# Gate A moved into earlier stages and two selection lists counted by ScalarE, in one inference step of a hybrid encoder

## The reference, cut to what matters

```python
mod = silu(c) @ w_ada + b_ada                       # 6 x 1024 values for each of two conditions
h = rms_norm(x) * (1 + sc1) + sh1
u, q, k, v, qi, ki, wi, gate_a, gate_b = split(h @ w_in)      # gate_a, gate_b: 1024 wide each
y_ssm = s5_scan(u, ...)                             # A: state space model
score = sum_h w[t,h] * relu(qi[t,h] . ki[s])        # indexer; the 256 highest keys of a query are kept
attn = attention over the keys kept                 # B
out_a = glu_val * sigmoid(glu_gate)                 # from gelu(y_ssm) @ w_glu
out_b = attn @ w_attn_out
x = x + g1 * ((sigmoid(gate_a)*out_a + sigmoid(gate_b)*out_b) @ w_out)
x = x + g2 * hier_moe(rms_norm(x) * (1 + sc2) + sh2)          # 16 experts, two for a token
```

## Time and profile before

| what | value |
|---|---|
| median of 3 runs | 1735.23 us (1731.95 to 1743.67) |
| the profiled execution's own time | 1734.8 us |
| its span, from the first to the last instruction | 1733.0 us |
| mean granted clock of TensorE | 0.92 |
| busy, of the span: TensorE / VectorE / ScalarE / GpSimd | 1460.3 / 886.4 / 336.5 / 169.5 us |
| moved to and from memory | 196.83 MB, mean 114 GB/s |

### The profile page before, as it was taken

The page is one execution under the profiler, slowest core; times in us unless marked ns, Lnnn a source line. Parts: engine busy times, 40 slices in busy tenths (PEclk is TensorE's granted clock), DMA queues, the critical chain, the costliest instruction groups (busy, mean ns, idle before and its releaser), DMA issues. The chain is left out here.

```text
span 1733.0 us, 18606 instructions
## 1 busy us (share of the span) xinstructions
PE 1460.3 (84%) x6385; PEld 814.6 (47%) x6386; DVE 886.4 (51%) x1799; ACT 336.5 (19%) x721; POOL 169.5 (10%) x356
## 2 busy tenths in 40 slices
PE   7799995978755999999988989989972899999870
PEld 1455541446422666666655666544442444444430
DVE  1322224977598989899985555323335111111117
ACT  3311111012462111111113556001110111111110
POOL 0000003020100111111110000000000122222220
PEclk9899997988966999999999999899985899999985
DMA  9200006640104222211004000432227366675728
GB/s 338 98 5 5 4 10 203 201 78 2 32 4 134 62 62 62 62 57 57 37 17 161 2 2 1 180 125 109 100 100 258 137 242 218 244 266 193 261 103 309
DMA packets 135629, 196.83 MB, mean 114 GB/s; under 512 B 27109, under 2 KB 102565, under 8 KB 135221
## 3 DMA queue, kind: packets, MB, share of 16 engines
q1 hardware_dynamic: 121634, 156.23, 27.4%
q0 software_dynamic: 9312, 28.59, 4.5%
q10 hardware_dynamic: 4612, 11.05, 1.8%
HBM read 154.81 MB, written 39.03 MB: 112 GB/s over the span
## 5 line engine op out<-in xcount | busy, mean ns | idle before, releaser
L1075 PE MATMUL ps<-hT,gt_w 128*128 128x352 f32 (+1 forms) x768 | 240.0, 471 | 18.9 <-DMA gt_w<-in_w_glu 18.9
L1109 DVE TENSOR_SCALAR_CACHE_REDUCE tk_hits<-sc,tk_cand 128x384 bf16<-128x384 f32 (+6 forms) x217 | 250.4, 1154 | 7.7
L1930 PE MATMUL ps<-ex_wgu,ex_xT 128*128 x416 | 191.1, 614 | 18.6 <-SPq L1845 10.7
L1075 PEld LDWEIGHTS ps<-hT,gt_w 128*128 128x128 f32 x768 | 146.8, 191 | 108.9 <-DMA gt_w<-in_w_glu 20.0
L1930 PEld LDWEIGHTS ps<-ex_wgu,ex_xT 128*128 128x128 f32 x416 | 79.4, 196 | 113.6 <-issue 113.6
L1490 PE MATMUL ps<-hT,mergedT 128*128 128x512 f32 (+1 forms) x288 | 120.3, 601 | 5.2 <-DMA op_wr<-in_w_route_expert 5.2
L1075 PE MATMUL ps<-zT,gt_w 128*128 128x352 f32 (+1 forms) x384 | 120.9, 468 | 0.0
L2003 DVE SCALAR_TENSOR_TENSOR ex_hid<-ex_silu,ex_weight,ps 128x256 f32<-128x256 f32 x26 | 12.5, 480 | 207.9 <-ACT ex_silu L1975 207.9
L1951 PE MATMUL ps<-ex_wd,ex_hidT 128*128 x208 | 93.6, 593 | 0.2 <-DVE ex_hidT L2010 0.2
L1075 PEld LDWEIGHTS ps<-zT,gt_w 128*128 128x128 f32 x384 | 73.0, 190 | 44.1
L1490 PEld LDWEIGHTS ps<-hT,mergedT 128*128 128x128 f32 (+1 forms) x288 | 50.9, 186 | 68.9 <-issue 63.0
(11 more groups left out here) (425 smaller groups left out, 1867.5 us busy)
## 6 DMA issues: line engine op xcount, KB each, us to landing
ex_wgu<-in_w_gate SPq DMA_DIRECT2D x16, 1024.0 KB, 5.9
ex_wgu<-in_w_up SPq DMA_DIRECT2D x16, 1024.0 KB, 11.1
ex_wd<-in_w_down SPq DMA_DIRECT2D x16, 1024.0 KB, 13.0
sp_ada_w<-in_w_ada SPq DMA_DIRECT2D x14, 1024.0 KB
gt_w<-in_w_in SPq DMA_DIRECT2D x16, 512.0 KB, 5.1
cb_y<-y_dram ACTq DMA_DIRECT2D x16, 512.0 KB, 8.5
merge_left_dram<-qiT SPq DMA_DIRECT2D x8, 544.0 KB, 6.2
mg_gb<-gate_b_dram SPq DMA_DIRECT2D x8, 544.0 KB, 3.7
```

Source lines behind the costliest of these rows:

```text
L1075: i = nc.tensor.matmul(m.ps[:, seq % 8, 0:n], w[:, c % NB, at + k, :], rhs[:, k, lo:lo + n], start=k == 0, stop=k == nk - 1)
L1109: return v.tensor_scalar(hits[0:r, 0:w], m.sc[0:r, c:c + w], scalar, 0.0, ALU.is_ge, ALU.add, accum_out=cnt[0:r, j:j + 1])
L1930: j = nc.tensor.matmul(m.ps[:, 2 + b, :], xT[:, b, k, :], wgu[:, bass.ds(at, 1), k, :].rearrange("p o n -> p (o n)"), start=k == 0, stop=k ...
```

## The change

Three parts.

1. Gate A. Column blocks 0 to 3 are worked out in `ssm_parameters`, 4 to 6 in `index_scores`, block 7 stays. A new class does it: SP loads the block's weights (512 KB), TensorE makes three spans of eight products, ScalarE copies each span from PSUM, GpSimd stores it in a new tensor in memory. The selection stage loads a block's 1088 columns again, and ScalarE takes their Sigmoid at once. To make room, the 16 modulation chunks use one PSUM bank, each as four groups of 64 columns on four strips of 32 partitions; the score groups of the index stage use seven banks, and TensorE waits with each group for all but three of the Relus before it. Half-products of four (one span is two halves) stand after 18 of the 25 score groups.

2. Selection. The lists are put in the order prompt blocks 3 to 7, block 2, sample; VectorE counts the first five, ScalarE the last two, by Sign(candidate - score) with a summing output, turned into a count by two one-column steps. Since a score that equals the candidate counts half there, the two thresholds are mended after the loop (`mended`). The loop of 31 is written out, counts don't wait for one another, and ScalarE makes the last scaling of each mask, after all its evacuations. Count i stands in ScalarE's list behind unit (6.5 i + 4) / 10.2.

3. Experts. The gate and up weights of a place are loaded when the gate and up products that used it are done, the down weights when the down products are.

The core of the diff, by stage and engine. In `ssm_parameters`, SP (the first load stands behind the five rows and log_dt, the second behind the loads of C and D) and GpSimd:

```diff
+                gates.load(sp, 0)
...
+                gates.load(sp, 1)
                 for i in range(2, len(ada)):
                     sp.wait_ge(aps, i - 1)
                     load_mod_weights(sp, i)
+                    if i == 7:
+                        gates.load(sp, 2)
+                    if i == 10:
+                        gates.load(sp, 3)
...
+                for s in range(len(gates.spans)):
+                    gates.store(pool, s)
+                gates.all_stored(pool)
```

TensorE there (`filler(spans, chunks)` takes a span of gate A and a chunk in turn):

```diff
+                def mod_chunk(i):
+                    pe.wait_ge(awl[i % 2], 32 * (i // 2 + 1))
+                    if i:
+                        pe.wait_ge(aev, i)
+                    for k in range(KD):
+                        for x in range(4):
+                            nc.tensor.matmul(m.ps[32 * x:32 * x + 2, 7, 0:AC // 4], m.cT[:, k, :],
+                                             aw[:, i % 2, k, AC // 4 * x:AC // 4 * (x + 1)], start=k == 0, stop=False)
+                    for x in range(4):
+                        j = nc.tensor.matmul(m.ps[32 * x:32 * x + 2, 7, 0:AC // 4], m.ones[DEC:DEC + 1, 0:2],
+                                             ab[:, i % 2, AC // 4 * x:AC // 4 * (x + 1)], start=False, stop=True)
+                    j.then_inc(aps, 1)
...
-                mod_chunks(range(0, 1))
+                filler(range(0, 1), range(0, 2))
                 pe.wait_ge(ldp, 1)
...
-                mod_chunks(range(1, 4))
+                filler(range(1, 5), range(2, 6))
...
-                mod_chunks(range(4, 8))
+                filler(range(5, 8), range(6, 10))
                 pe.wait_ge(wtr, 1)
                 input_matrices(range(0, 6))
-                mod_chunks(range(8, 12))
+                filler(range(8, 12), range(10, 13))
                 pe.wait_ge(bbr, 1)
                 input_matrices(range(6, 8))
...
                     if x == 2:
-                        mod_chunks(range(12, len(ada)))
+                        filler((), range(13, len(ada)))
```

ScalarE copies in the same order, each chunk's row in four parts: span 0 and chunks 0 and 1 ahead of its Exp and Sin, all others behind them. VectorE waits ahead of the decay table, whose place holds the weights of gate A until then:

```diff
+                dve.wait_ge(gates.psum, len(gates.spans))
                 step(v.tensor_copy(m.decay[:, :, :], bc(m.r8[:, :], 2, COLS)))
```

The new class (its `copy` on ScalarE waits for the products and for the store two spans before; its `store` on GpSimd waits for the copy):

```diff
+class GateSpans:
...
+    def load(self, engine, u):
+        if u >= 2:
+            engine.wait_ge(self.psum, 3 * (u - 1))
+        c = OFF_GA + self.columns[u] * P
+        engine.dma_start(self.w[:, u % 2, :, :], self.src[:, :, c:c + P]).then_inc(self.loaded[u % 2], 16)
+
+    def products(self, pe, s, bank, part=range(KD)):
+        _, lo, n = self.spans[s]
+        if part[0] == 0:
+            if s % 3 == 0:
+                pe.wait_ge(self.loaded[(s // 3) % 2], 16 * (s // 6 + 1))
+            if s:
+                pe.wait_ge(self.copied, s)
+        for k in part:
+            i = self.nc.tensor.matmul(self.m.ps[:, bank, 0:n], self.w[:, (s // 3) % 2, k, :], self.m.hT[:, k, lo:lo + n],
+                                      start=k == 0, stop=k == KD - 1)
+        if part[-1] == KD - 1:
+            i.then_inc(self.psum, 1)
```

In `index_scores`, SP and TensorE:

```diff
+        halves, quads = 2 * len(gates.spans), len(steps) // 4
+        half_after = {4 * ((x + 1) * quads // (halves + 1)) + 3: x for x in range(halves)}
...
                 sp.dma_start(m.vs[:, 0:CB, :], A.cache_v[0].rearrange("(b p) d -> p b d", p=P)).then_inc(ld, 16)
+                gates.load(sp, 0)
+                gates.load(sp, 1)
                 sp.wait_ge(m.fst, 64)
...
-                    if n % 4 == 0 and n >= 8:
-                        pe.wait_ge(rl, n - 4)
+                    if n % 4 == 0 and n >= 4:
+                        pe.wait_ge(rl, n - 3)
...
+                    if n in half_after:
+                        x = half_after[n]
+                        gates.products(pe, x // 2, 7, range(KD // 2 * (x % 2), KD // 2 * (x % 2 + 1)))
```

In `select_keys_and_gates`, ScalarE (`gates(u)` evacuates the three or four parts of unit u):

```diff
+                def count(i):
+                    act.wait_ge(cr, i + 1)
+                    for x in range(2):
+                        r, c, w, mc = lists[V + x]
+                        nc.scalar.activation(m.mask[0:r, mc:mc + w], m.sc[0:r, c:c + w], ACT.Sign, scale=-1.0,
+                                             bias=cand[0:r, V + x:V + x + 1].bitcast(F32),
+                                             accum_out=signs[0:r, x:x + 1]).then_inc(sg, 1)
+                    act.wait_ge(sg, 2 * i + 2)
+                    for x in range(2):
+                        k = nc.scalar.activation(cnt[:, V + x:V + x + 1], signs[:, x:x + 1], ACT.Identity,
+                                                 bias=middle[:, x:x + 1], scale=-0.5)
+                    k.then_inc(sc_, 1)
+
+                for u in range(len(units)):
+                    gates(u)
+                    for i in counts_after[u]:
+                        count(i)
+                for j, (r, c, w, mc) in enumerate(lists):
+                    act.wait_ge(mk_, j + 1)
+                    nc.scalar.activation(m.mask[0:r, mc:mc + w], m.mask[0:r, mc:mc + w], ACT.Copy, scale=-NEG).then_inc(done, 1)
```

VectorE's iteration there, in place of the hardware loop (the candidates count for ScalarE as soon as `cr` says so, and its counts come back by `sc_`):

```diff
+                for i in range(BITS):
+                    v.tensor_tensor(cand[:, :], thr[:, :], bit[:, :].broadcast_to([P, NL]), ALU.bitwise_xor).then_inc(cr, 1)
+                    dve.wait_ge(cr, i + 1)
+                    v.tensor_scalar(bit[:, :], bit[:, :], 1, None, ALU.logical_shift_right)
+                    for j in range(V):
                         r = lists[j][0]
+                        k = count(j, cand[0:r, j:j + 1].bitcast(F32))
+                    dve.wait_ge(sc_, i + 1)
+                    step_loop(k)
+                    step_loop(v.tensor_scalar(take[:, :], cnt[:, :], TOPK - 0.5, None, ALU.is_ge))
+                    step_loop(v.copy_predicated(thr[:, :], take[:, :], cand[:, :]))
```

In `experts`, SP:

```diff
-                    sp.wait_ge(dn, used)
-                    load_expert(nc, sp, m, A, e)
+                    sp.wait_ge(gp, used)
+                    load_gate_up(sp, m, A, e)
+                    sp.wait_ge(dn, used)
+                    load_down(sp, m, A, e)
```

285 lines of the change are left out of this document (191 added, 94 removed).

## The result

The changed kernel takes 1663.53 us (median of four runs, 1659.36 to 1666.19) against 1733.59 us before (four runs, 1727.65 to 1743.67): a ratio of 0.958, 95% interval 0.955 to 0.961. The forecast was 1686, its range 1650 to 1722. The profiled execution took 1666.19 us; its span fell by 68.8 us, from 1733.0 to 1664.2.

| stage | before, us | after, us | difference | forecast |
|---|---|---|---|---|
| up to the parameters | 266.0 | 267.1 | +1.1 | 0 |
| parameters | 105.9 | 131.1 | +25.2 | +38 |
| scan | 88.4 | 100.7 | +12.3 | 0 |
| index | 81.9 | 96.6 | +14.7 | +12 |
| selection | 367.5 | 268.4 | -99.1 | -93 |

The account below looks back on a forecast made before the run. Key selection was taken as bound by TensorE and VectorE, both full side by side. Selection -93, parameters +38, index +12 and experts -6 sum to -49: 1734.8 - 49 = 1686 us, range 1650 to 1722.

Parts of the forecast that it names:

- 6.05: Selection: VectorE's loop iteration after the change, in us, 31 times, against 9.63 before.
- the pace by ScalarE's order: Selection: later iterations follow ScalarE's queue of counts behind evacuations, 6.25 us each.
- the tail: Selection: time from the loop's end to the next stage, 61 us against 57.0 before.
- Rival (e): Selection: the VectorE and ScalarE hand-over goes wrong, loop not below 8 us; 1735, no change; chance 0.04.
- rival (c): Selection: Sign and Sigmoid take turns loading tables; about +10, 1696, or 1726 with the drain; chance 0.10.
- the 275 taken: Parameter stage: TensorE's product 0 starts at 275 us, when its weights land; bounds 273.7 and 278.
- I take 2.5: Parameter stage: a narrow modulation chunk on TensorE takes 2.5 us, between 1.8 and 4.1.
- Rival (d): Parameter stage: narrow products run load and matmul in series, 10.5 us a chunk; +104, 1790; chance 0.05.
- rival (b): Index stage: TensorE keeps its half clock, +41 instead of +12; 1715; chance 0.09.
- The rest: Index stage, after the first stall: TensorE has 76 us of work against VectorE's 73, so +3.
- Two of these, 1459.32 - 1458.28 = 1.04 us, now go out before the down product ends: 6 x 1.04.: Experts: two of three load issues ahead of SP's signal go out earlier, giving -6 us; bounds 0 and -10.7.
- rival (a): Parameter and index stages: idle room takes nearly everything, parameters +12, index +3; 1651; chance 0.12.

Follow-up runs that it names:

- the ring alone: The kernel before with only the experts' part of the change (gate and up weights and down weights loaded at separate times): 1713.76 us, ratio 0.989.
- the run with the counts early: The changed kernel with ScalarE's counts placed by VectorE's pace, ahead of evacuations, and five mask scalings behind units 19 to 23: 1655.12 us.

## Why the prediction was right, and where it was not

- **Both engines of the selection must be relieved, and are: right.** -99 against -93. The iteration was a little shorter than 6.05 (5.54), the pace by ScalarE's order behind the first two iterations a little faster than 6.25 ((804.04 - 626.89) / 29 = 6.11, from the third candidate on), the first wait 8.36 us (8 forecast), the loop 5 us shorter than forecast, the tail 59.9 (61). The run with VectorE alone relieved shows that this would not have done (2.7 us). That TensorE alone would not have done was not run by itself; the run with all lists on VectorE shows that the stage then follows VectorE's list, 323 us. One reading was off: 0.45 us for Sign over 384 columns is more than 2.06 in proportion (0.37), and the pass took 0.62; a whole count took 3.3 us, near the 3.5 taken. Rival (e), a loop that does not get below 8 us, fell with the 6.46 on average.
- **Sign and Sigmoid take turns at tables, rival (c): fell.** One load of 1.28 us in the stage. The Trainium skill's "ScalarE: Activation LUTs", "Table sets: the hidden batching unit", does not name Sign among the functions that are in every set; here it behaves as one of them.
- **The parameter stage: right mechanism, mis-sized chunk.** +25 against +38. The order on TensorE does decide, and VectorE's wait for the last input matrices is the price. VectorE's first read came to the tenth of a microsecond, but only because a start 3.4 us later than the 275 taken was made up for by two shorter chunks and a first product of 6.94 us (7.7 taken). The term "I take 2.5" for a chunk measured 1.3; 11 chunks between the read and those matrices make 13 us, about the whole error. The lower bound of 1.8, from the router's 0.025 us a product, was not low enough: these start 0.016 us apart, and the starts in the earlier trace rows, rounded to 0.1 us, allow anything from 0.013 to 0.027. The changes between wide and narrow form, for which 0.7 was added, cost some 0.2 us at most: a product of 352 columns beside such chunks takes 4.93 us to the next start, beside wide chunks the same 4.93, and in the selection 4.74. By the rule of the Trainium skill, "TensorEngine Tiling (Array Packing)", section "Key Properties", the chunk should have come nearer to 4.1; that is what the wide form takes, not the narrow one. Rival (d), 10.5 us a chunk, is far off.
- **The index stage: right.** The arrival of the weights (10.2 us after the start), the idle time (9.12 against 8.7) and the clock (0.91, so not rival (b)) came out. The rest is 5.6 us and not 3.
- **The experts: the failed step is "Two of these, 1459.32 - 1458.28 = 1.04 us, now go out before the down product ends: 6 x 1.04."** It took the third issue for fixed, which took 1.72 us behind two others and takes 0.37 alone; and it left out that TensorE's products ran slower behind each wait. The 22 us, shown by the ring alone, lie beyond its bound of -10.7 too.
- **The scan: no term at all.** The sum took the stages that the change does not touch for fixed. The 12.3 us are the difference of two draws of the clock, 88.4 and 100.7, and the instructions of either kernel gave a short scan and a long one (88.4 and 99.7; 88.3 and 100.7). What decides a draw stays open.
- **The sum.** -49 came out as -68.8: experts -16, parameters -13, selection -6, index +3, scan +12, start +1, and -1 in the combine. Without the long draw of the scan it would be -81, a kernel near 1651 us: below the forecast's own 1660 to 1707, and at the edge of its range. That is rival (a)'s time too, but not by its parts: it had +12 in the parameters and +3 in the index, where +25 and +15 came. So the way and the main term were right by their mechanism, but that the number lies well inside the range is in part luck: the scan, which the forecast did not know of, took back part of what the experts and the chunks gave beyond it.

## What to carry to other kernels

Where two engines fill a stage side by side, price each engine's list from end to end, and relieve both: here VectorE's relief alone gave 2.7 us, TensorE's with a somewhat shorter VectorE list 44.5, both 99. When a signal stands behind several DMA issues on one queue, count the whole row of issues up to the signal, and add the slower products that follow each wait of TensorE. And before a stage's difference is explained, look at the clock of that stage in more than one profile: here a stage with short waits on TensorE differed by 12 us between executions of the same instructions, and spare products in those waits took most of that away in three profiles (86.1 to 89.9 us), at a gain of 2 us at most against a short draw.

## What the runs showed of the hardware that was not expected

- Matmul instructions of 64 columns on four column strips start 16 ns apart (64 in 1.0 us), and a chunk costs a third of the wide form, 1.3 against 4.1 us.
- The scan's TensorE clock is 0.73 to 0.86 for the same instructions, its time 88.3 to 100.7 us; behind a wait of 3.49 us products took 1.23 us and not 0.71. With 18 or 22 spare products of 0.69 us each in the waits the stage took 86.1, 86.6 and 89.9 us, at a clock of 0.90 to 0.95.
- Sign needed no table load beside Sigmoid, before it or after it: 62 Signs and one load of 1.28 us in the stage, and in the run with the counts early none ahead of the first Sign.
- A 1 MB load's issue on SP took 0.37 us alone, 0.76 to 1.72 us as the third in a row.
